# A mixture-of-experts decoder layer on one core: the table of routed sums as two halves, two scatters for a block, and the second copy of y ahead of the transpose

## What is computed

```python
def body(acc, blk):
    toks, bw, e = blk
    xb = hp[toks]
    yb = (jax.nn.silu(xb @ w_gate[e]) * (xb @ w_up[e])) @ w_down[e]
    return acc.at[toks].add(yb.astype(f32) * bw[:, None]), None
...
shared = (jax.nn.silu(hf @ ws_gate) * (hf @ ws_up)) @ ws_down
return (acc[:n_tok] + shared.astype(f32)).astype(h.dtype).reshape(bsz, seq, dm)
```

## Time and profile before

| | |
|---|---|
| median of 3 runs | 2586.3 us (2585.36 to 2596.59) |
| the profiled execution: its own time | 2587.75 us |
| its span, first to last instruction | 2585.9 us |
| PE busy | 2391.2 us, 92% |
| DVE busy | 1759.7 us, 68% |
| POOL busy | 927.3 us, 36% |
| granted TensorE clock, mean over the span | 0.965 of full speed |
| the 79 turns from 903.46 to 2470.21 us | 1566.75 us, 61% of the span |

### The profile page before, as it was taken

One profiled execution on the slowest core, in us unless ns is written; L12 is line 12 of the kernel. 1 busy time (PEld: TensorE's weight loads), 2 busy tenths in 40 slices (PEclk: granted clock), 3 DMA queues, 4 the chain that ended last, 5 costly groups with the idle time before them and its releaser, 6 DMA issues. The chain is left out here.

```text
span 2585.9 us, 49372 instructions
## 1 busy us (share of the span) xinstructions
PE 2391.2 (92%) x11266; PEld 1917.0 (74%) x11268; DVE 1759.7 (68%) x2382; ACT 1180.8 (46%) x1863; POOL 927.3 (36%) x755
## 2 busy tenths in 40 slices
PE   8899999899988799999999999999899998999986
PEld 6677777688867677777777777777777776777875
DVE  6676777768778676566756666766676666766548
ACT  3525353522327454445544445545454444544334
POOL 0010000011110445454445454444544545545537
PEclk9999999899989899999999999999999998999999
DMA  6232322565664688778887878978887778887873
GB/s 244 84 134 104 107 92 89 161 237 192 238 212 142 229 261 242 217 217 242 259 251 214 230 208 246 275 213 255 245 247 217 210 203 250 260 243 208 223 226 132
DMA packets 160576, 533.83 MB, mean 206 GB/s; under 512 B 30817, under 2 KB 55553, under 8 KB 140033
## 3 DMA queue, kind: packets, MB, share of 16 engines
q1 hardware_dynamic: 107248, 346.12, 38.3%
q0 software_dynamic: 52656, 186.88, 29.5%
q10 hardware_dynamic: 608, 0.02, 0.0%
HBM read 386.61 MB, written 146.34 MB: 206 GB/s over the span
## 5 line engine op out<-in xcount | busy, mean ns | idle before, releaser
L2625 PE MATMUL psG<-gu_split,xT_hi 128*128 x2624 | 630.7, 393 | 3.4 <-ACT xT_hi L2399 1.9
L2625 PEld LDWEIGHTS psG<-gu_split,xT_hi 128*128 128x128 f32 x2624 | 499.2, 190 | 110.0 <-issue 4.1
L2384 POOL DMA_INDIRECT acc<-y,si x162 | 312.8, 1931 | 683.7 <-DMA acc<-y,si 432.6
L1652 POOL DMA_INDIRECT xg<-hcut,gi x332 | 395.8, 1192 | 105.4 <-issue 97.8
L2639 PE MATMUL psG<-gu_split,xT_lo 128*128 x1304 | 341.2, 403 | 0.5 <-issue 0.5
L2504 DVE TENSOR_TENSOR gu_split<-raw_gu,gu_split (+1 forms) x127 | 290.1, 2284 | 57.5 <-ACT gu_split L2422 46.9
L2488 DVE STREAM_TRANSPOSE xF<-xg 128x1024 f32<-128x1024 f32 x82 | 175.4, 2139 | 216.6 <-DMA xg<-hcut,gi 216.6
L2677 PE MATMUL psY<-d_hi,HT_hi 128*128 x648 | 215.5, 415 | 65.5 <-DVE y L2580 61.6
L2639 PEld LDWEIGHTS psG<-gu_split,xT_lo 128*128 128x128 f32 x1304 | 233.0, 188 | 43.1 <-issue 0.6
L2422 ACT ACTIVATE gu_split<-raw_gu x126 | 234.5, 1909 | 29.8 <-issue 18.1
L2677 PE MATMUL psY<-d_hi,HT_lo 128*128 x648 | 217.1, 418 | 29.0 <-DVE HT_lo L2567 28.9
(11 more groups left out here) (401 smaller groups left out, 3944.8 us busy)
## 6 DMA issues: line engine op xcount, KB each, us to landing
raw_gu<-in_w_gate_dram SPq DMA_DIRECT2D x64, 1024.0 KB, 5.2
raw_gu<-in_w_up_dram SPq DMA_DIRECT2D x64, 1024.0 KB, 9.6
raw_d<-in_w_down_dram SPq DMA_DIRECT2D x64, 1024.0 KB, 6.6
wring<-split_d SPq DMA_DIRECT2D x24, 1024.0 KB, 4.8
split_d<-wring POOLq DMA_DIRECT2D x8, 1024.0 KB, 4.2
raw_d<-mixed SPq DMA_DIRECT2D x16, 512.0 KB, 5.9
xt<-in_x_dram SPq DMA_DIRECT2D x16, 512.0 KB, 5.8
htab<-h SPq DMA_DIRECT2D x16, 512.0 KB, 2.7
```

The source lines that it names most:

```text
L1652: nc.gpsimd.indirect_dma_start(out=to[:, g, 0:PIECE], out_offset=None, in_=hcut.rearrange("r a w -> (r a) w"), in_offset=bass.IndirectOffs ...
L2384: nc.gpsimd.indirect_dma_start(out=acc, out_offset=bass.IndirectOffsetOnAxis(ap=si[k][:, 0:1], axis=0), in_=y[k][:], in_offset=None, compu ...
L2625: nc.tensor.matmul(psG[slot][:], xT_hi[slot][:, c, :], right[:, bass.ds(w, 1), c, :].rearrange("p a n -> p (a n)"), start=(n == 0 and c == ...
```

## The change

The table `acc` becomes two tables, `acc[0]` and `acc[1]`, of 2176 rows by 512 columns. Whatever wrote or read a row of the old one is now two DMAs of 512 columns each: `store_kept`, `store`, the zero rows and `load_z`, with counts of 32 where 16 stood. A block's scatter becomes two scatters of half rows. The first waits for ACT's copy alone and for the first half of the scatter before; the second for DVE's copy and for the second half of the scatter before. `added` has a semaphore for each half and each buffer; DVE's copy waits for its own half, ACT's index `si` for both. On DVE the call of `turn_x` in the first block moves from ahead of the gate split to behind the copy of `y`.

```diff
@@ -1269,7 +1269,8 @@
 
             def store_kept(n):
                 sp.wait_ge(kept_s, n - EARLY + 1)
-                sp.dma_start(acc[n * P:(n + 1) * P, :], kept[:]).then_inc(kept_out[n % 2], 16)
+                for hf in range(2):
+                    sp.dma_start(acc[hf][n * P:(n + 1) * P, :], kept[:, hf * 512:(hf + 1) * 512]).then_inc(kept_out[n % 2], 16)
 
             def store_hT(n):
                 sp.wait_ge(hT_s, n + 1)
...
@@ -1779,7 +1780,8 @@
 
             def store(n):
                 sp.wait_ge(out_s, n + 1)
-                sp.dma_start(acc[n * P:(n + 1) * P, :], out[n % 2][:]).then_inc(acc_out[n % 2], 16)
+                for hf in range(2):
+                    sp.dma_start(acc[hf][n * P:(n + 1) * P, :], out[n % 2][:, hf * 512:(hf + 1) * 512]).then_inc(acc_out[n % 2], 16)
 
             load_hT(2)
             load_hT(3)
...
@@ -2379,10 +2382,11 @@
                     for h in range(2):
                         s.wait(pool, y_s[h])
 
-                    pool.wait_ge(added[1 - k], (s.turn + k) * 16)
-                    carry_wait(pool, passed)
-                    nc.gpsimd.indirect_dma_start(out=acc, out_offset=bass.IndirectOffsetOnAxis(ap=si[k][:, 0:1], axis=0),
-                                                 in_=y[k][:], in_offset=None, compute_op=ALU.add).then_inc(added[k], 16)
+                        pool.wait_ge(added[h][1 - k], (s.turn + k) * 16)
+                        carry_wait(pool, passed)
+                        nc.gpsimd.indirect_dma_start(out=acc[h], out_offset=bass.IndirectOffsetOnAxis(ap=si[k][:, 0:1], axis=0),
+                                                     in_=y[k][:, h * 512:(h + 1) * 512], in_offset=None,
+                                                     compute_op=ALU.add).then_inc(added[h][k], 16)
 
             nt = turns(pool, body)
             for k in range(2):
...
@@ -2413,8 +2417,9 @@
                     nc.scalar.activation(gi[0][:], idx[:, bass.ds(s.n + AHEAD, 1)], ACT.Copy).then_inc(next_gi_s, 1)
 
             def scatter_index(s, k):
-                act.wait_ge(added[k], s.turn * 16)
-                carry_wait(act, passed)
+                for h in range(2):
+                    act.wait_ge(added[h][k], s.turn * 16)
+                    carry_wait(act, passed)
                 nc.scalar.activation(si[k][:], idx[:, bass.ds(s.n, 1)], ACT.Copy).then_inc(si_s, 1)
 
             def high(src, dst, done):
...
@@ -2572,12 +2577,12 @@
                         pair_weight(nexts[n + 1], s.turn + 2, 0)
                         pair_weight(nexts[n], s.turn + 1, 1)
                     product(s.n + 2, 1 - k, s.turn + 1 + k)
+                    when_first(dve, nexts[n + 1], lambda: split(nexts[n + 1], 0))
+                    s.wait(dve, yps_s[1])
+                    dve.wait_ge(added[1][k], s.turn * 16)
+                    nc.vector.tensor_copy(y[k][:, 512:], psY[:, 1, :]).then_inc(y_s[1], 1)
                     if k == 0:
                         turn_x(s.turn + 2)
-                    when_first(dve, nexts[n + 1], lambda: split(nexts[n + 1], 0))
-                    s.wait(dve, yps_s[1])
-                    dve.wait_ge(added[k], s.turn * 16)
-                    nc.vector.tensor_copy(y[k][:, 512:], psY[:, 1, :]).then_inc(y_s[1], 1)
                     when_first(dve, nexts[n + 1], lambda: split(nexts[n + 1], 1))
                     when_first(dve, nexts[n], lambda: split(nexts[n], 2))
 
...
@@ -2794,7 +2799,8 @@
         @block.sync
         def _(sp):
             def load_z(t):
-                sp.dma_start(z[:, t, :], acc[t * P:(t + 1) * P, :]).then_inc(z_in[t], 16)
+                for hf in range(2):
+                    sp.dma_start(z[:, t, hf * 512:(hf + 1) * 512], acc[hf][t * P:(t + 1) * P, :]).then_inc(z_in[t], 16)
 
             def load_hT(n):
                 sp.wait_ge(hTlo_s, n - EARLY - HT_AHEAD + 1)
...
@@ -2809,8 +2815,9 @@
 
             nt = sp.value_load(n_turns[0:1, 0:1], min_val=0, max_val=BLOCKS // TURN)
             for k in range(2):
-                sp.wait_ge(added[k], nt * (16 * TURN // 2))
-                carry_wait(sp, passed)
+                for h in range(2):
+                    sp.wait_ge(added[h][k], nt * (16 * TURN // 2))
+                    carry_wait(sp, passed)
             for g in range(LATE):
                 for t in (2 * g, 2 * g + 1):
                     if t < EARLY:
...
@@ -3107,7 +3114,7 @@
     htab = nc.dram_tensor("htab", [ROWS, ROW_W], F).ap()
     hcut = nc.dram_tensor("hcut", [ROWS, QUADS, PIECE], F).ap()
     hT_d = nc.dram_tensor("hT_d", [TILES, P, KC, P], F).ap()
-    acc = nc.dram_tensor("acc", [ROWS, D], F).ap()
+    acc = [nc.dram_tensor(f"acc{i}", [ROWS, D // 2], F).ap() for i in range(2)]
     with ExitStack() as ctx:
         def sb(name, shape, dt=F):
             return ctx.enter_context(nc.sbuf_tensor(name, shape, dt))
...
@@ -3149,7 +3156,7 @@
         shared_in = ctx.enter_context(nc.semaphore("shared_in"))
         hT_in = [ctx.enter_context(nc.semaphore(f"hT6_in{i}")) for i in range(HT_AHEAD)]
         kept_out = [ctx.enter_context(nc.semaphore(f"kept_out{i}")) for i in range(2)]
-        added = [ctx.enter_context(nc.semaphore(f"added{i}")) for i in range(2)]
+        added = [[ctx.enter_context(nc.semaphore(f"added{h}{i}")) for i in range(2)] for h in range(2)]
 
         row_out = [ctx.enter_context(nc.semaphore(f"row_out{i}")) for i in range(2)]
         hT_out = [ctx.enter_context(nc.semaphore(f"hT_out{i}")) for i in range(2)]
```

More of the change, by code:

```diff
@@ L1361, in keep @@
                 if n > EARLY:
-                    act.wait_ge(kept_out[(n - 1) % 2], 16 * ((n - 1 - EARLY) // 2 + 1))
+                    act.wait_ge(kept_out[(n - 1) % 2], 32 * ((n - 1 - EARLY) // 2 + 1))
                 nc.scalar.activation(kept[:], h[n % 2][:], ACT.Copy, scale=ALPHA).then_inc(kept_s, 1)
@@ L1792, in _ @@
                 sp.dma_start(hcut[SEQ:ROWS, a], zeros[:, 0:PIECE]).then_inc(pads_out, 16)
-            sp.dma_start(acc[SEQ:ROWS, :], zeros[:]).then_inc(pads_out, 16)
+            for hf in range(2):
+                sp.dma_start(acc[hf][SEQ:ROWS, :], zeros[:, 0:512]).then_inc(pads_out, 16)
             load_hT(4)
@@ L1806, in _ @@
             for k in range(2):
-                sp.wait_ge(kept_out[k], 16 * (TILES - EARLY) // 2)
+                sp.wait_ge(kept_out[k], 32 * (TILES - EARLY) // 2)
                 sp.wait_ge(wt_out[k], 48 * TILES // 4)
-            sp.wait_ge(pads_out, 48 + 16 * QUADS)
+            sp.wait_ge(pads_out, 64 + 16 * QUADS)
         @block.gpsimd
@@ L1815, in _ @@
                 pool.wait_ge(hT_out[k], 16 * TILES // 2)
-                pool.wait_ge(kept_out[k], 16 * (TILES - EARLY) // 2)
+                pool.wait_ge(kept_out[k], 32 * (TILES - EARLY) // 2)
             nc.gpsimd.memset(zeros[:], 0.0).then_inc(zeroed, 1)
             nc.clear_and_free_semaphores(spent)
-            pool.wait_ge(pads_out, 48 + 16 * QUADS)
+            pool.wait_ge(pads_out, 64 + 16 * QUADS)
             for k in range(2):
@@ L1929, in finish @@
                 if n >= 2:
-                    dve.wait_ge(acc_out[n % 2], 16 * (n // 2))
+                    dve.wait_ge(acc_out[n % 2], 32 * (n // 2))
                 elif n == 0:
-                    dve.wait_ge(pads_out, 48 + 16 * QUADS)
+                    dve.wait_ge(pads_out, 64 + 16 * QUADS)
                 nc.vector.scalar_tensor_tensor(out=out[n % 2][:], in0=h[n % 2][:], scalar=ALPHA,
@@ L2046, in _ @@
                 dve.wait_ge(hT_out[k], 16 * TILES // 2)
-                dve.wait_ge(kept_out[k], 16 * (TILES - EARLY) // 2)
+                dve.wait_ge(kept_out[k], 32 * (TILES - EARLY) // 2)
             low(2)
@@ L2363, in _ @@
             for k in range(2):
-                pool.wait_ge(acc_out[k], 16 * EARLY // 2)
+                pool.wait_ge(acc_out[k], 32 * EARLY // 2)
             def body(i):
@@ L2549, in _ @@
             for k in range(2):
-                dve.wait_ge(acc_out[k], 16 * EARLY // 2)
+                dve.wait_ge(acc_out[k], 32 * EARLY // 2)
             pair_weight(block0, 1, 0)
@@ L2782, in z_ready @@
             if t < EARLY:
-                eng.wait_ge(z_in[t], 16)
+                eng.wait_ge(z_in[t], 32)
             else:
@@ L2977, in add_shared @@
                 dve.wait_ge(y_s, n - EARLY + 1)
-                dve.wait_ge(z_in[n], 16)
+                dve.wait_ge(z_in[n], 32)
                 nc.vector.tensor_tensor(z[:, n, :], z[:, n, :], psY[:].rearrange("p a b -> p (a b)"), ALU.add).then_inc(sum_s, 1)
```

## The result

The changed kernel takes 2627.8 us (median of four runs, 2620.7 to 2631.6), the one before, run beside it, 2590.6. The ratio is 1.014, with a 95% interval of 1.0103 to 1.0177: **slower**, by 37 us or 1.4%, clear of the noise and above the 2599 us from which the prediction calls it slower. The forecast was 32 us less. The profiled execution took 2631.0 us with a span of 2629.1, 43.2 more than before at nearly the same mean clock (0.967 and 0.965).

A forecast was written before the change was run, and what follows sets the result against it. PE was taken as the bound, stalled by DVE work standing behind late gathered pieces. 2587.75 + 44 - 104 + 24 + 4 = 2556, and 2554 us since that execution lay 1.5 above the median; range 2510 to 2650.

The forecast's parts named there:

- What bounds the kernel: PE, 92% busy, idle 95 us in 79 routed turns, waiting for DVE's copy of y (61.6) and HT_lo (28.9).
- The rule of 9.2 us: In a routed turn: it ends 9.2 us after HT_lo starts, if HT_lo is late and the clock stays up.
- Part 1: Gate turns (36, gate and up weights split in the first block): turn_x behind the copy makes HT_lo later, +44 us.
- Part 2: Down turns (26, only down weights split in the first block): the copy no longer waits for the pieces, -10 us.
- Part 3: Two scatters a block: halves land sooner, so pieces come earlier; 26 turns splitting only down weights take 18.0 each, -104 us.
- Part 4: PE's clock falls in half of the 36 gate turns, at 1.3 us each: +24 us, between 0 and 101.
- Part 5: The rest: the last scatter comes 1.9 us later and load_z issues 16 more DMAs, +4 us, between 0 and 10.
- The first rival: On POOL's queue the pieces land no sooner; down turns give 10 us, not 104: 2648 us, chance 0.22.

The follow-up runs named there:

- turn_by_kind: Kernel before, with the transpose ahead of the gate split where block n + 2 begins a new expert, behind the copy of y elsewhere: 2580.7 us, ratio 0.9968.
- pool_first: Kernel before with the transpose moved behind the copy of y, plus two gathers of 16 bytes a row behind the first block's scatter alone: 2671.5 us, ratio 1.036.
- move_only: Kernel before, one table and one whole scatter, with only DVE's transpose moved behind the copy of y: 2596.6 us, ratio 1.0035.
- copy_early: Kernel before, with DVE's copy of y ahead of the gate split; transpose ahead of it in turns with that split, behind it elsewhere: 2551.6 us, ratio 0.9854.

## Why the prediction was wrong

The time lies inside the stated range of 2510 to 2650 us, but on the other side of no change.

- **What bounds the kernel** was read rightly in part. The rule of 9.2 us held wherever HT_lo was late and the clock stayed up. What the earlier trace rows showed as POOL's 432.6 us was taken as waiting that smaller scatters would shorten; it was a ring, in which each scatter waits for the one before, with a fixed phase against the gate load. In most gate turns that ring, and not DVE alone, gave the 19.9 us. The earlier trace rows hid it, since its landings (6.4 us) are those of second blocks; those of first blocks had a median of 9.6.
- **Part 1** (+44) was right: 27 gate turns with the clock up take 20.3 each, forecast 20.4, which makes +42 for 36.
- **Part 2** (the move, -10 in down turns) was mis-sized: with whole scatters it is -52. Its own term, the copy's 0.6 us, is what turn_by_kind tries: -3. It missed that the transpose, put between copy and up split, also widens the distance in gate turns from the first block's scatter to SP's gate load, which waits for the up split: from some 1.3 to 3.9 us.
- **Part 3** (-104) is the step that failed. On top of the move the second scatter gave no gain in down turns, but took back 40 of 52 us. The step that went wrong is the sentence that a first half goes out while POOL waits, so that the second issue is hidden. The first half was the one that waited: at 1335.60, 3.79 us for the second block's first half, which was issued at 1325.33 behind the four pieces and landed 9.5 us later. Behind that wait stand two issues where one stood, and the pieces go at -6.1 as before. The 1.63 us for an issue was right (1.58). "Lands in 5.0" was right for the first block (5.0 and 5.6) and wrong for the second (8.1 and 7.5). pool_first prices 2.5 us in the place of the second issue alone at 84 us.
- The rule of the Trainium skill, DMA: Bandwidth & Descriptors, in "Anatomy of one DMA — SWDGE (gpsimd) path", a fixed cost for each such DMA and little for its bytes, gives 2.6 us for a half, an estimate from that page, and 0.6 less than for a whole. The least in the rows is 4.9 for a half and 6.1 for a whole, 1.2 apart. If the other half of the bytes costs as much, 3.7 of the 6.1 us don't go with the bytes: the runs agree with the rule's direction, and with neither of its figures.
- **Part 4** (+24): the clock fell in 9 of 36 gate turns, not 18, by 1.5 to 2.3 us each: +16. In down turns it fell 15 times instead of 17.
- **Part 5** (+4): -1.6 outside the turns.
- **The first rival** (2648, chance 0.22) is what happened, by its own mark: the last piece's issue ends (1347.02) after the gate load (1345.37), and in move_only before it (1341.43 and 1343.79). The mark is not sharp: in copy_early's turn of 18.47 us the last piece ends 0.4 us after the load. The rival was 19 us too high against the profiled execution (2649.8 to 2631.0): the clock 8, the rest 6, the gate turns, the other turns and the down turns some 2 each. That its 10 us in down turns met the measured 11 is luck: it has the copy's 0.6 us there, while the runs show 52 gained by the move and 40 lost by the second scatter.

## What to carry to other kernels

On a queue that many wait for, price a further issue by what stands behind it: the same 2.5 us of POOL cost 84 us ahead of the pieces and nothing ahead of the whole rows. Such prices need not add up: both together cost 162. An issue is hidden by a wait only if it stands ahead of that wait. Where stages stand in a ring of waits for landings, moving the order on one engine can be worth more than making a transfer smaller: here 52 us against 26 in down turns. Ask also which transfers a row of landings holds, before its median is used for others. Split such a change into its halves before judging it: here one of them shortened down turns, and an order found from it is 1.8% faster than the kernel before.

## What was not expected of the hardware

- An indirect scatter of half rows takes POOL as long to issue as one of whole rows (1.58 and 1.63 us), and a gather of 16 bytes a row as long as one of 1088 (0.95 at least, for both).
- A whole scatter lands in 6.1 us at best, and in 11.7 to 12.3 when the gate load is issued 1.2 to 1.7 us behind it on another queue. Its first packet then starts 6.1 us after its issue (1229.12) instead of 2.2 (1221.96). Cutting either megabyte of the load to an eighth takes a little over 1 us off; what makes the rest of the delay is not shown.
- PE's clock, after stalls of about 2.2 us, fell in some gate turns and not in others whose HT_lo was as late: 1589.37 at 1.00, 1609.68 at 0.92, HT_lo at +11.11 in both. Some of the second turn ran at 1.2 instead of 2.4 GHz. No row here tells them apart.
